# Moving the router, the row positions and the row scatter into the Fourier stage, and turning the rows inside the experts

## The reference, cut to what matters

```python
y = fourier_mix(hx, o_w_o)                       # 2-D DFT per channel group, real part, then @ w_o
x = x + ga_m * rmsnorm(y, g_mix_post)
t = modulate(rmsnorm(x, g_ffn_pre), sh_f, sc_f)
logits = t @ w_router                            # (2048, 8)
top_v, top_i = top_k(logits, 2); gates = softmax(top_v)
xs = t[tokens sorted by expert]                  # 4096 rows
h = silu(ragged_dot(xs, w1)) * ragged_dot(xs, w3)
y = ragged_dot(h, w2) * gates                    # expert width 3584
x = x + ga_f * rmsnorm(sum of each token's two rows, g_ffn_post)
```

## Time and profile before

| what | value |
|---|---|
| median of 3 runs | 10352.59 us (10346.6 to 10357.9) |
| the profiled execution | 10354.85 us |
| its span, first to last instruction | 10353.3 us |
| mean granted TensorE clock | 0.958 of full speed |
| PE busy | 93% of the span |
| first expert matmul | 4757.73 us from the span's start |

### The profile page before, as it was taken

One profiled execution on the slowest core, in us unless ns is written; L12 is line 12 of the kernel. 1 busy time (PEld: TensorE's weight loads), 2 busy tenths in 40 slices (PEclk: granted clock), 3 DMA queues, 4 the chain that ended last, 5 costly groups with the idle time before them and its releaser, 6 DMA issues. The chain is left out here.

```text
span 10353.3 us, 132234 instructions
## 1 busy us (share of the span) xinstructions
PE 9606.0 (93%) x51264; PEld 6592.2 (64%) x51265; DVE 2678.0 (26%) x5594; ACT 1827.1 (18%) x3634; POOL 280.3 (3%) x388
## 2 busy tenths in 40 slices
PE   9975999999999998937999999999999999999995
PEld 3443677544444443416878878878788788788784
DVE  1136444333222236322111111111111111111113
ACT  1123233210000002312111111111111111111112
POOL 0010000010000000010000000000000000000002
PEclk9986999999999999957999999999999999999997
DMA  5312000260000002375221111122221211211124
GB/s 202 122 46 81 3 5 5 85 233 19 19 19 19 25 25 102 106 239 177 97 80 61 61 67 49 49 73 76 78 70 61 75 57 59 77 61 61 68 99 177
DMA packets 488344, 798.23 MB, mean 77 GB/s; under 512 B 23998, under 2 KB 366446, under 8 KB 481346
## 3 DMA queue, kind: packets, MB, share of 16 engines
q1 hardware_dynamic: 448680, 642.41, 18.4%
q0 software_dynamic: 39456, 152.81, 3.9%
HBM read 612.86 MB, written 182.29 MB: 77 GB/s over the span
## 5 line engine op out<-in xcount | busy, mean ns | idle before, releaser
L2562 PEld LDWEIGHTS ex_psH<-ex_xt,ex_w 128*128 128x128 f32 x32256 | 3694.4, 193 | 397.5 <-issue 397.5
L2562 PE MATMUL ex_psH<-ex_xt,ex_w 128*128 x32256 | 3717.9, 276 | 117.1 <-issue 80.8
L2572 PE MATMUL ex_psY<-ex_w,ex_a 128*128 128x512 f32 x4032 | 1814.5, 593 | 6.2 <-DVE ex_a L2626 6.2
L2626 DVE TENSOR_TENSOR ex_a<-ex_s,ex_psH 128x128 f32<-128x128 f32 x1008 | 289.1, 287 | 4567.9 <-PE ex_psY L2572 3234.0
L577 PE MATMUL de_ps<-de_ht,de_w 128*128 128x512 f32 x2816 | 1222.9, 592 | 0.0
L2572 PEld LDWEIGHTS ex_psY<-ex_w,ex_a 128*128 128x128 f32 x4032 | 727.6, 190 | 730.7 <-issue 730.7
L2616 ACT ACTIVATE ex_s<-ex_psH 128x128 f32<-128x128 f32 x1008 | 279.9, 278 | 4492.3 <-PE ex_psH L2562 4492.3
L577 PEld LDWEIGHTS de_ps<-de_ht,de_w 128*128 128x128 f32 x2816 | 534.9, 190 | 672.5 <-issue 672.5
L2616 ACT ACT_TABLE_LOAD x504 | 646.6, 1283 | 86.2 <-DVE ex_a L2626 9.5
L593 PE MATMUL de_ps<-de_w,de_a 128*128 128x512 f32 x1408 | 622.2, 595 | 18.0 <-DVE hx_h L743 18.0
L2636 DVE TENSOR_TENSOR ex_ya<-ex_psY,ex_ya 128x512 f32 x936 | 602.5, 684 | 25.4 <-PE ex_psY L2572 25.4
(11 more groups left out here) (324 smaller groups left out, 4675.8 us busy)
## 6 DMA issues: line engine op xcount, KB each, us to landing
ex_w<-in_o_w SPq DMA_DIRECT2D x336, 1024.0 KB, 7.7
en_ch<-in_w_mod SPq DMA_DIRECT2D x48, 1024.0 KB, 4.9
de_w<-in_e_w SPq DMA_DIRECT2D x66, 512.0 KB, 5.4
xs<-de_zero POOLq DMA_DIRECT2D x44, 512.0 KB, 30.2
ys<-de_zero POOLq DMA_DIRECT2D x44, 512.0 KB, 30.9
tr_x<-xs SPq DMA_DIRECT2D x44, 512.0 KB, 4.8
xst<-tr_ht SPq DMA_DIRECT2D x44, 512.0 KB, 4.9
ex_xt<-xst POOLq DMA_DIRECT2D x36, 512.0 KB, 7.2
```

The lines of the kernel that those rows point to most:

```text
L2562: last = nc.tensor.matmul(psH[:, h, q * P:(q + 1) * P], W[:, s, k, h * P:(h + 1) * P], XT[:, k, bass.ds(at, P)], start=k == 0, stop=k == K ...
L2572: last = nc.tensor.matmul(psY[:, c], A[:, h], W2[:, s, h, c * BANK:(c + 1) * BANK], start=h == 0, stop=h == HU - 1)
L2626: nc.vector.tensor_tensor(A[:, h], S[:, h], psH[:, h, P:2 * P], ALU.mult).then_inc(a_done, 1)
```

## The change

The stages `router`, `positions`, `spread` and `transpose_rows` are gone, and with them the stores of xn and ht, the counts in DRAM and the reloads.

In `fourier`, PE's work of a block is interleaved with the routing of the tiles of block o-2. HT is now read in place. Y has eight buffers in place of four.

```diff
+            def logits(o):
+                for n, i in enumerate(range(FIRST[o], FIRST[o + 1])):
+                    for k in range(KD):
+                        last = nc.tensor.matmul(psA[:, 0, n * NE:(n + 1) * NE], HT[i % 2][:, k], WR[:, k], ...)
+            def ranks(o):
+                for n, i in enumerate(range(FIRST[o], FIRST[o + 1])):
+                    nc.tensor.matmul(psA[:, 1, n * NE:(n + 1) * NE], TRI[:, :], M[:, o % 2, n], start=True, stop=False)
+                    last = nc.tensor.matmul(psA[:, 1, n * NE:(n + 1) * NE], ONE[:, :], MS[:, i], start=False, stop=True)
+            def period(o):                     # PE
+                turn = list(range(FIRST[o - 1], FIRST[o])) if o else []
+                minus(o, 0)                    # V of half 0
+                if o >= 2:
+                    logits(o - 2)
+                plus(o, 0)                     # U of half 0
+                minus(o, 1)
+                if o >= 2:
+                    ranks(o - 2)
+                if turn:
+                    transposes(turn[0])
+                plus(o, 1)
+                for i in turn[1:]:
+                    transposes(i)
...
+            def period(o):                     # DVE
+                if o >= 2:
+                    route(o - 2)               # copy, max, max_index, cast, one-hots, sums; waits l_done
+                combine(o, 0)
+                if o >= 2:
+                    place(o - 2)               # one-hot x rank, row sum, cast to POS; waits r_done
+                if turn:
+                    modulate(turn[0], o - 1)
+                combine(o, 1)
+                for i in turn[1:]:
+                    modulate(i, o - 1)
...
+            gather(0)                          # POOL
+            gather(1)
+            for o in range(9):
+                if o >= 2:
+                    scatter(o - 2)             # 2 indirect DMAs a tile, waits pos_made
+                if o + 2 < 9:
+                    gather(o + 2)
+            scatter(7)
+            scatter(8)
```

In `experts` the rows are loaded untransposed, one tile ahead, by ACT's DMA queue, and turned within the first chunk of each expert:

```diff
+            def turn(row):                     # PE, 8 transposes
+                pe.wait_ge(x_in, row * 16 + 16)
+                pe.wait_ge(ht_a, row); pe.wait_ge(ht_v, row)
+                for k in range(KD):
+                    last = nc.tensor.transpose(psT[...], X[:, k * P:(k + 1) * P], ident[:, :])
...
+                    with pe.Fori(1, nb) as j:
+                        if first:
+                            turned(b0 + j)     # waits ht_a, ht_v of this row tile
                         up(b0, s, 0, j, lo + j)
+                        if first:
+                            turn(b0 + j + 1)
                         down(s, lo + j - 1, final)
                         up(b0, s, 1, j, lo + j)
...
+            def take(row):                     # ACT; DVE has the same for the other four
+                act.wait_ge(tr_done, row + 1)
+                load(row + 1)                  # reads TI, issues the DMA of the next row tile into X
+                act.wait_ge(x_used, row + 1)
+                for k in range(4, 8):
+                    last = nc.scalar.activation(XT[:, k, ...], psT[:, 1, ...], ACT.Identity, bias=..., scale=...)
...
-            return (row % HB).with_bounds(min_val=0, max_val=HB - 1)
+            return (row % XB).with_bounds(min_val=0, max_val=XB - 1)      # HB = 16, XB = 17
```

More of the change, by code:

```diff
@@ L381, in _ @@
                     norm(n + 2)
[L384 to L407, removed]
 def dense(nc, mix_d, w_o, x0_d, gate0, cols, w1, w3, w2, gate1, x1_d, x2_d, ident_d, HX, clear):
@@ L1844, in _ @@
                 third(ch)
+            pe.wait_ge(f_out, PA + PB + PC)
             for o in range(4, 8):
-                outputs(o)
-                turn(o)
+                period(o)
             channels(2)
-            outputs(8)
-            turn(8)
-            turn(9)
+            period(8)
+            logits(7)
+            for i in range(FIRST[8], FIRST[9]):
+                transposes(i)
+            ranks(7)
+            logits(8)
+            ranks(8)
+            pe.wait_ge(pos_made, 9)
+            nc.tensor.matmul(psA[:, 1, 0:NE], ONE[:, :], MS[:, NT], start=True, stop=True).then_inc(total_done, 1)
         @block.scalar
@@ L1928, in _ @@
             modulate(8)
+            act.wait_ge(gap_made, 1)
+            nc.scalar.activation(GG[:, 1], GG[:, 0], ACT.Exp).then_inc(gate_exp, 1)
         @block.vector
@@ new lines, in modulate, with settle @@
+            def modulate(i, o):
+                dve.wait_ge(tr_done, i + 1)
+                if o:
+                    dve.wait_ge(l_done, o)
+                for k in range(4):
+                    last = nc.vector.tensor_scalar(HT[i % 2][:, k], psT[:, 0, k * P:(k + 1) * P], mod[:, 1, k:k + 1],
+                                                   mod[:, 0, k:k + 1], ALU.mult, ALU.add)
+                last.then_inc(ht_v, 1)
+            steps = [0]
+            def settle(ins):
+                ins.then_inc(step, 1)
+                steps[0] += 1
+                dve.wait_ge(step, steps[0])
@@ new lines, in place @@
+            def place(o):
+                i, n = FIRST[o], FIRST[o + 1] - FIRST[o]
+                dve.wait_ge(r_done, o + 1)
+                for t in range(n):
+                    for k in range(2):
+                        last = nc.vector.tensor_tensor(TMP[:, t, k], ON[:, o % 2, t, k], psA[:, 1, t * NE:(t + 1) * NE], ALU.mult)
+                settle(last)
+                settle(nc.vector.reduce_sum(PF[:, 0:n], TMP[:, 0:n], AXX))
+                nc.vector.tensor_copy(POS[:, :, i:i + n], PF[:, 0:n].rearrange("p t k -> p k t")).then_inc(pos_made, 1)
@@ L2251, in spread @@
[L2251 to L2277 removed]
+            route(7)
@@ L2621, in _, with take @@
             dve.sem_inc(y_added, 4)
-            dve.wait_ge(counts_in, 16)
+            dve.wait_ge(const_in, 32)
+            def take(row):
+                dve.wait_ge(tr_done, row + 1)
+                dve.wait_ge(x_used, row + 1)
+                at = dve.snap(place(row) * P) if not isinstance(row, int) else row * P
+                for k in range(4):
+                    last = nc.vector.tensor_scalar(XT[:, k, bass.ds(at, P)], psT[:, 0, k * P:(k + 1) * P], mod[:, 1, k:k + 1],
+                                                   mod[:, 0, k:k + 1], ALU.mult, ALU.add)
+                last.then_inc(ht_v, 1)
             def hidden0(h, n):
```

633 lines of the change are left out of this document (241 added, 392 removed).

## The result

The changed kernel takes 10118.2 us (median of 4 runs, 10115.0 to 10121.8) where the kernel before took 10355.2: a ratio of 0.9770, 95% interval 0.9753 to 0.9787. The forecast was 10113 us, range 10065 to 10220. The profiled execution after took 10121.75 us (span 10120.1), that of before 10354.85, so 233.1 us are to be found in the traces, against 239 in the forecast's sum.

A forecast was written before the change was run, and what follows sets the result against it. PE, busy 93% of the span, was taken as the bound. 294 us gained up to the first expert product, 55 lost in the experts: -239 from 10354.85 gives 10116, less 2.3 for the median: 10113 us, range 10065 to 10220.

The forecast's parts named there:

- clearing 130 tiles each: Ahead of Fourier: 172 more stores of 512 KB to clear the scratch, taken as 0 us.
- (1): Fourier blocks: routing work lengthens a block of two tiles from 19.84 to 21.7 us; +14 us in all, 0 to +52.
- (2): Tail of the Fourier stage, from the last normalisation to the experts' first DMA: 27 us in series, ends 20 and 45.
- (3): Start of the experts, from their first DMA to the first product: 17 us, ends 13 and 24.
- (4): Experts: transposes in PE's full queue, waits ahead of them and changes of expert cost +55 us, ends 34 and 130.
- The two waits for ACT: Fourier blocks: two new waits for ACT to empty a bank, estimated at about 1 us each.
- Waits and register work ahead of the turns: Experts: estimated at 0.25 us for each unit of the first chunk, 9 us.
- change-of-expert term: Experts: at seven changes of expert PE waits for DVE, held by the stores before; 1 us each, 7 us.
- late-row rival: Experts: with one x buffer the row's load comes late, 3 us for each of 36 turns, 108 us: 10221; chance 12%.
- Inner fetches: Experts: a first-chunk loop body leaves its instruction window, 4.28 us for each of 36 row tiles: +154, 10267; chance 4%.
- Routing not hidden: Fourier blocks: the added DVE and PE work falls one behind the other, +52 us instead of +14: 10151; chance 10%.
- Ring of 17: Experts: the remainder by 17 in each of 1008 `up` costs PE 0.3 us: +302, 10415, slower than before; chance 6%.

The follow-up runs named there:

- e2: The changed kernel with the short logit products issued four at a time between the U products of a block's first half: 10099.0 us.
- e7: e3 with the loops over experts of PE and DVE written out as well: 10085.7 us.
- e11: The changed kernel with a ring of 16 places for turned rows instead of 17: 10123.6 us.
- e10: The changed kernel with one edit, POOL storing each row tile of y as soon as its last sum is made: 10083.6 us.
- e9: The changed kernel with spread logits, moved y wait, PE's, DVE's and ACT's expert loops written out, reordered tail, and y stored early: 10030.9 us.
- e3: The changed kernel with DVE's wait for the free y buffer moved behind the first take of turned rows and first hidden parts: 10088.0 us.
- e4: The changed kernel with PE's loop over the eight experts written out: 10129.7 us.
- e6: The kernel before with only the new Fourier stage; old turning stage, each tile looked up in a table by SP, and old experts: 10267.0 us.

## Why the prediction was right, step by step

The mechanism was right: the standing stages went, and what came back was a longer Fourier stage, a tail and PE's turns. That the sum is only 6 us off is luck: misses of +25 and of -19 us cancel in it.

| step | forecast | measured |
|---|---|---|
| ahead of Fourier (run to run, no edit) | 0 | +3.8 |
| clearing 130 tiles each | 0 | 0 |
| (1) Fourier's start to block 0 | +1 | +1.0 |
| (1) blocks 0 to 8 | +13 | +26.8 |
| last U product to last normalisation | 0 | -1.1 |
| (2) tail, to the experts' first DMA | 27 | 33.2 |
| (3) from there to the first product | 17 | 14.1 |
| (4) experts | +55 | +39.8 |
| `finish` | 0 | +0.9 |

- **(1), mis-sized.** Block 0's start to the last U product took 209.7 us before and 236.6 after. The logits' own price, 0.109 us each, lay inside my bounds near the upper one; with the ranks 4.3 us a block where I took 3.6. What I had no term for is the clock behind them: 1.5 to 1.8 us in four blocks, 3.0 in one, 9.7 in all, and 0.9 more in the later bursts themselves, which take up to 4.05 us where the first take 3.63. e2 shows it by its absence, and with e2 the block, 22.24 us, is within 0.6 of the forecast 21.7. That DVE keeps pace was right: PE waits nowhere for DVE in the blocks. The two waits for ACT, put at 1 us each from no row, took 0.78 and 0.56.
- **(2), mis-sized.** From the last normalisation to the first scatter I had 15.2 us and it took 18.8. I priced the last logits at 3.6 us though my own rows had this stretch at half clock (+3.4), and the ranks likewise (1.9 against 0.7); the other terms were 1.0 less. The other 2.7 us lie behind the last scatter, where I carried over 6.7 us and it took 9.4: POOL's drain took 3.97 us in place of 2.67, the landing 0.4 more, and three clears of semaphores in place of one about 1 us. DVE's table ran beside the scatters as I had it, but only just: its operations on 48 elements take 0.20 to 0.50 us, not 0.19, and it was done 0.3 us ahead of POOL's last wait.
- **(3)** The first x row was 6.5 us in landing, inside the bounds, and the first weights, not the row, end the last wait (3.21 us).
- **(4), mis-sized.** A turn costs 0.88 us in the queue, not the 1.06 that its own row shows, whose two ends overlap the products ahead and behind (6.5 us less for 36 turns), and I had counted the 37th, which stands ahead of the first product, here as well as in (3). Waits and register work ahead of the turns, 9 us in the sum from no row, cost nothing. The change-of-expert term was right in kind and in sum, 7 forecast and 7.8 more behind DVE measured, though not as 1 us each. The landing was 3.6 us in the median and 6.5 at most, so the late-row rival never came near.
- **Signs named beforehand.** Blocks of 21 to 22 us: 24.05. First expert product near 4464: 4483.85. Turns without idle time ahead, and steady units of 10.58 us: both so. The 70 us from the last U product to the first expert product don't follow from the forecast's own terms, which give 56; it was 58.
- **Rivals.** Inner fetches: none. Late x row: none, until e7 brought PE to the row 6 us sooner. Routing not hidden: 13.8 of its 38 added us came, but most of them by the clock and none by the loop through two engines. Ring of 17: e11.

DVE's wait of 13.44 us I had seen only as a price of the turns, and not as a cost that can be taken away. e10 shows that it was worth 35 us in the changed kernel. The kernel before has it too, at all seven changes, 124 us of DVE's time, with 12.1 us of PE's behind it; no run took it away there.

Left open: why F starts up to 16 us apart from one execution to another, what the 5 us in e2's experts are, and why block 4 keeps its clock.

## What to carry to other kernels

When a stage is folded into a full one, price the neighbours of the new instructions too: a burst of very short products cost its own 3.5 us and, in five blocks of six, half its length again in the long products behind it; dealt out among them it cost only itself. Where an idle time is taken away and the run doesn't get shorter, look what the freed engine now meets: here PE met the y buffer and the x row, both behind stores that were held to the end of an expert, and one edit on the idlest engine released most of it. Give a buffer back piece by piece, as e9 does. And put a wait directly ahead of the first write that needs it: e3 stopped one multiply short of that, and e7 showed PE waiting there. That last step no run tried.

## What the runs showed of the hardware

- PE without a gap is not PE at full clock: behind 3.5 us of eight-column products the granted clock was 0.68 for 5.3 us (in five of six blocks), behind two bursts of 1.8 us with 4.7 us of long products between them too, and 1.00 with the same 32 mixed in.
- The same instructions at the same place ran at either level in different executions (the V products of block 8, 5.27 or 3.67 us): a 3.3 us step in F to E that is no edit's.
- ACT's table loads in the experts fell from 503 to 36 (46.2 us), although modulations with another function came in: the loop of units without a turn now has none, while before each unit had one. Both are off the path.
- POOL's drain at the end of a stage was 3.97 us long behind the Fourier stage after (the same in e4 and e9) and 2.67 behind the old scatter, and every engine waited for it.
- The stores of y, three to six of 512 KB right behind each other, were 9.4 us in landing in the median and 14.0 at most; a load of the same size on ACT's queue 3.6 and 6.5. Beside stores and weights (e7) such a load took 7.0 to 9.3.
- A look-up by SP, which reads one number of a table into a register, took 0.93 us in the median (e6, 44 of them), ahead of each load.
